# A three-block sequence model on one core: the softmax steps of two attention stages in another order

## The reference, cut to what matters

```python
# sparse attention (nsa_mixer): three softmaxes per head over three kinds of keys
s_c = einsum(q, kc) * scale - slopes * dist_c         # 63 compressed keys, each of 32 tokens
p_c = masked_softmax(s_c, c_end <= t);   o_cmp = p_c @ vc
s   = einsum(q, k_slc) * scale - slopes * dist        # selected keys: the top 16 of 16 blocks, so all up to t
p   = masked_softmax(s, dist >= 0);      o_slc = p @ v_slc
s_w = einsum(q, k_win) * scale - slopes * dist        # window: the last 512 tokens
p_w = masked_softmax(s_w, mask);         o_win = p_w @ v_win
o   = g0 * o_cmp + g1 * o_slc + g2 * o_win

# differential attention (diff_mixer): two softmaxes per head, one per half of the query and key channels
s = einsum('bqhid,bkhid->bhiqk', q, k) * scale - slopes * dist     # i = 0, 1
p = masked_softmax(s, dist >= 0)
a = p[:, :, 0] - lam * p[:, :, 1];       o = a @ v
```

## Time and profile before

| | value |
|---|---|
| three runs, median | 4952.93 us |
| the profiled execution | 4949.35 us, span of the trace 4947.4 us |
| busy in the span: PE, DVE, ACT, POOL | 87%, 38%, 27%, 22% |
| stage nsa in the trace | from 507.8 (first S) to 726.2 (end of the last result) |
| stage diff in the trace | from 753.8 to 943.3 |
| steps in them | 4 x 24 and 4 x 16 |

### The profile page before, as it was taken

One profiled execution on the slowest core, in us unless ns is written; L12 is line 12 of the kernel. 1 busy time (PEld: TensorE's weight loads), 2 busy tenths in 40 slices (PEclk: granted clock), 3 DMA queues, 4 the chain that ended last, 5 costly groups with the idle time before them and its releaser, 6 DMA issues. The chain is left out here.

```text
span 4947.4 us, 55759 instructions
## 1 busy us (share of the span) xinstructions
PE 4315.8 (87%) x21602; PEld 3528.5 (71%) x21602; DVE 1857.7 (38%) x3257; ACT 1335.4 (27%) x2341; POOL 1088.4 (22%) x544
## 2 busy tenths in 40 slices
PE   8997888869983888669999999999899999956897
PEld 6886666757772777456887887888688888845675
DVE  3031565662475665225234234000033333345432
ACT  3120322342213444312000003112143444442121
POOL 2220001241231655211222221221111111122320
PEclk9997999969996999889999999999999999968898
DMA  3233101221323110211111112332243342265422
GB/s 118 100 137 84 35 18 43 76 94 35 137 94 130 37 39 25 82 43 38 57 43 51 44 43 77 113 130 81 87 100 89 107 108 82 82 207 160 143 82 81
DMA packets 277875, 412.06 MB, mean 83 GB/s; under 512 B 52853, under 2 KB 187894, under 8 KB 272122
## 3 DMA queue, kind: packets, MB, share of 16 engines
q1 hardware_dynamic: 206010, 298.36, 19.7%
q10 hardware_dynamic: 69424, 105.53, 5.9%
q0 software_dynamic: 2192, 4.80, 0.4%
HBM read 285.66 MB, written 122.95 MB: 83 GB/s over the span
## 5 line engine op out<-in xcount | busy, mean ns | idle before, releaser
L136 POOL TENSOR_TENSOR weights_wlow<-weights_raw,weights_whigh 128x1024 fp32r<-128x1024 f32 (+1 forms) x236 | 668.0, 2852 | 2582.0 <-ACT weights_whigh L127 2582.0
L260 PE MATMUL acc<-h_high_half,weights_whigh 128*128 128x512 f32 x1440 | 566.3, 393 | 81.0 <-POOL weights_wlow L136 69.2
L127 ACT ACTIVATE weights_whigh<-weights_raw 128x1024 fp32r<-128x1024 f32 (+1 forms) x236 | 267.4, 1163 | 1294.0 <-PE acc L260 653.2
L260 PE MATMUL acc<-h_high_half,weights_wlow 128*128 128x512 f32 x1440 | 564.3, 392 | 0.0
L260 PE MATMUL acc<-h_low_half,weights_whigh 128*128 128x512 f32 x1440 | 564.3, 392 | 0.0
L260 PEld LDWEIGHTS acc<-h_high_half,weights_whigh 128*128 128x128 f32 x1440 | 273.2, 190 | 142.7 <-POOL weights_wlow L136 70.9
L3158 PE MATMUL acc<-h_high_half,weights_whigh 128*128 128x512 f32 x768 | 332.3, 433 | 0.0
L263 PE MATMUL acc<-weights_whigh,h_high_half 128*128 128x512 f32 x768 | 303.4, 395 | 13.9 <-PEq L189 13.9
L260 PEld LDWEIGHTS acc<-h_high_half,weights_wlow 128*128 128x128 f32 x1440 | 273.4, 190 | 56.5
L260 PEld LDWEIGHTS acc<-h_low_half,weights_whigh 128*128 128x128 f32 x1440 | 272.7, 189 | 57.3
L3158 PE MATMUL acc<-h_low_half,weights_whigh 128*128 128x512 f32 x768 | 302.9, 394 | 0.0
(11 more groups left out here) (526 smaller groups left out, 8094.7 us busy)
## 6 DMA issues: line engine op xcount, KB each, us to landing
weights_raw<-w_cols SPq DMA_DIRECT2D x94, 512.0 KB, 4.9
weights_raw<-w_ff SPq DMA_DIRECT2D x64, 512.0 KB, 3.8
weights_raw<-w_rows SPq DMA_DIRECT2D x30, 1024.0 KB, 7.2
att<-gated_result_sb SPq DMA_DIRECT2D x96, 130.0 KB, 2.3
weights_raw<-w_out SPq DMA_DIRECT2D x24, 512.0 KB, 3.8
cols<-cols1p_out ACTq DMA_DIRECT2D x40, 256.0 KB, 2.1
rows<-rows1p_out ACTq DMA_DIRECT2D x32, 256.0 KB, 2.6
x<-x_here SPq DMA_DIRECT2D x2, 4096.0 KB, 14.4
```

Source lines behind the costliest of these rows:

```text
L127: self.core.nc.scalar.activation(high[p][:, half * (KC // 2):(half + 1) * (KC // 2), :], raw[half], ACT.Copy).then_inc(self.core.sem("roun ...
L136: self.core.nc.gpsimd.tensor_tensor(low[p][:, hs, :], raw[half], high[p][:, hs, :].bitcast(F32), ALU.subtract).then_inc(self.core.sem("wei ...
L260: mm = nc.tensor.matmul(core.acc[b][:, :], wt[p][:, k, c * P:(c + 1) * P], h[:, k, half * HALF:(half + 1) * HALF], start=first, stop=final)
```

## The change

Only the two lists of steps are put in another order; every step stays as it was, and so does `attention`. In nsa the list becomes s0, c0, w0, s1, c1, w1, ..., s7, c7, w7: tile by tile, with selected, compressed and window keys in turn. In diff it becomes a0, b0, a1, b1, ..., a7, b7.

```diff
@@ nsa_attention, steps(p)
                                pieces=1, out=lambda it, t=t: [att[t * P:(t + 1) * P, ds(it * HD, HD)]]))
-            for t in range(NT):
+                st.append(dict(queries=q[p][:, t * P:(t + 1) * P], keys=[(kT["cmp"][:, :], 0)],
+                               masks=[(unseen[:, t, :], 0)], width=P, values=[(0, P, val["cmp"][:, :])],
+                               scale=HD ** -0.5, valid=valid[:, 0:1] if t == 0 else None,
+                               pieces=1, out=lambda it, t=t: [att[t * P:(t + 1) * P, ds(it * HD + 8 * HD, HD)]]))
                 t0 = max(0, t - 4)
                 w = (t + 1 - t0) * P
                 st.append(dict(queries=q[p][:, t * P:(t + 1) * P],
...
-            for t in range(NT):
-                st.append(dict(queries=q[p][:, t * P:(t + 1) * P], keys=[(kT["cmp"][:, :], 0)],
-                               masks=[(unseen[:, t, :], 0)], width=P, values=[(0, P, val["cmp"][:, :])],
-                               scale=HD ** -0.5, valid=valid[:, 0:1] if t == 0 else None,
-                               pieces=1, out=lambda it, t=t: [att[t * P:(t + 1) * P, ds(it * HD + 8 * HD, HD)]]))
             return st
@@ diff_attention, steps(p)
-            for i in range(2):
-                for t in range(NT):
+            for t in range(NT):
+                for i in range(2):
                     w = (t + 1) * P
```

## The result

The changed kernel took 4970.45 us (median of 9 runs, 4964.14 to 4974.97), the kernel before in the same rounds 4954.18 (9 runs, 4945.42 to 4957.02): 1.0032 times the time, 95% interval 1.0021 to 1.0042, so 16 us slower, 10 to 21. 4964 was forecast, with 4956 to 4975 as the range, and slower as the likeliest.

What follows compares the result with a forecast made beforehand. TensorE's work plus its waits was taken to bound both stages: nsa +15.2, diff -0.5, half-speed stretches -2, sum +12.7 us on 4949.35, that is 4962.0, or 4965.6 for a median; 4964.0 was given, range 4956 to 4975.

Steps and rivals of the forecast that it cites:

- The rule of covers: Both stages: TensorE waits by how much a step's softmax chain exceeds neighbouring steps' TensorE work; new nsa idle 9.6 us an iteration.
- T(s7): Transposes of nsa's last, widest selected step: chain 2.90 us against cover 1.22, so a wait of 1.68 us.
- T(s0): Transposes of nsa's first selected step, in the new order: a wait of 0.71 us.
- The old idle time: TensorE's idle time in nsa before the change, which the new order removes: 5.8 us an iteration (5.1 to 6.6).
- the 0.7 for store waits: nsa's compressed run before: waits for stored results, taken as 0.7 us an iteration beyond other waits, going away.
- diff: Differential attention stage: idle 2.1 us an iteration before, 2.0 to 2.1 after; net -0.5 us for four (-2 to +1).
- The half-speed stretches: After starts and loop turns at 1.2 GHz, slower matmuls grow into new idle time: 0.5 us each, -2 (0 to -4).
- The gain of the compressed run: Rival: the end of each nsa iteration gets faster and decides, 20 us in all, giving 4933 us; chance 0.04.
- Cancelling: Rival: gains and losses nearly cancel across store waits, half-speed stretches and chains: +5, 4954 to 4958 us; chance 0.17.
- The clock: Rival: waits in every nsa tile drop the clock once an iteration, adding 8 to 12 us: 4972 to 4976; chance 0.09.
- The signs: New trace: nsa exponential waits from 12.7 to some 30 us, no stored-result waits, iteration some 4 us longer, diff's within 0.3.
- signs of being wrong: Last three selected steps' transposes start without waits over 1 us, clock falls mid-iteration, or a stage after 945 us moves.

Runs made afterwards that it cites:

- e7: The kernel before (old order) with four result tiles in place of two: 4945.03 against 4953.08 us, ratio 0.9981.
- e2: The kernel before with the new order in diff alone: 4953.06 against 4951.88 us, ratio 1.0003.
- e9: The changed kernel with four result tiles in place of two: 4965.51 us against 4951.50 for the kernel before, ratio 1.0028.
- e1: The kernel before with the new order in nsa alone: 4967.51 against 4951.88 us, ratio 1.0032.
- e3: The kernel before with nsa's selected and window steps tile by tile, compressed steps as one run at the end: 4954.02 against 4951.88 us, ratio 1.0006.
- e5: The kernel before, with the row maximum of selected steps reading every fourth score: 4951.80 against 4953.08 us, ratio 1.0000.
- e8: The kernel before with nsa tile by tile as selected, window, compressed: 4958.43 against 4953.08 us, ratio 1.0013.
- e6: The changed kernel, with the row maximum of selected steps reading every fourth score: 4956.44 us, ratio 1.0007 to the kernel before.
- e10: Both stages with wide steps beside wide ones, plus four result tiles: 4927.83 us against 4951.50 for the kernel before, ratio 0.9953.
- e4: The kernel before with both stages reordered, wide steps beside wide ones: 4929.58 against 4951.88 us, ratio 0.9953.

## Why the prediction was right, point by point

*The rule of covers* held to within 0.1 us at each step, and to 0.02 from T(s3) to T(s7). Idle time in the fourth iteration, from one start to the next, with the forecast behind it: T(s1) 0.61 (0.67), T(s2) 0.72 (0.80), T(s3) 0.95 (0.93), T(s4) 1.08 (1.06), T(s5) 1.21 (1.19), T(s6) 1.45 (1.44), T(s7) 1.70 (1.68), T(s0) 0.78 (0.71), T(w7) 0.35 (0.32), M(w7) 0.75 (0.66). With 0.19 at T(c0) the sum is 9.8 us, where 9.6 was said.

*The old idle time* was sized too high at 5.8 us. Summed the same way the fourth iteration before has some 5.4, and its length says so too: 57.35 us with 9.8 idle leaves 47.55 of work, and 52.9 less 47.55 is 5.4. The second iteration, 52.6, has 5.1 by the same sum, in which 2 us at half speed stand as well. The term that was off is the 0.7 for store waits that was added to the 5.1. e7 shows that these waits are worth more, 1.5 to 1.7 us an iteration (52.6 and 52.9 against 51.17), but also that nearly all of it had already been counted in the 5.1, which was read from rows that have these waits in them: without them 51.17 less 47.55 leaves 3.6. So an iteration lengthened by 4.7 and 4.4 where +3.8 was forecast and +4.5 was the upper bound. The four iterations of nsa lengthened by 4.2, 4.7, 3.9 and 4.4, in sum 17.2, where +15.2 and a share of the -2 stood. The mechanism was right and the total came out some 4 to 5 us too low (+12.7 against +16 by the medians and +18.1 in the two stages), inside a range that was wide enough for it.

*diff*: -0.5 forecast, within -2 to +1; +0.9 in the trace, and no difference in e2. "The same within 0.3" for an iteration was a little too strict: the second lasts 0.6 longer, 46.0 us, and holds one wait of 1.2 us for a stored result, which the kernel before doesn't have there.

*The half-speed stretches.* The iterations with the start and the first turn in them grew by some 0.4 to 0.8 us less than the plain ones (+4.2 and +3.9 against +4.7 and +4.4), about the 0.5 each that was said. But the two traces don't have equal stretches at half speed: 3.9 us at the start and 10.2 around the turn before, 6.4 and 3.4 in the changed kernel, so this agreement may be luck. A cleaner pair is e7 and e9, with 3.4 us behind the turn in both: the third iteration, with the turn, grew by 5.4 us (55.70 to 61.11) and the plain ones by 6.2. The 0.8 less fits slower matmuls that grow into the idle time. At the start no pair has equal stretches. In diff nothing of the kind is seen.

*The rivals.* The gain of the compressed run is real, 5.1 to 5.4 us an iteration with what hangs on it, but 9.8 us came in its place. Cancelling didn't come. The clock did not fall in mid-iteration in any trace of this order (the changed kernel, e1, e9); what it did elsewhere stands in the last section.

*The signs.* Those of the waits came as written: 30.9 us for exponentials, T(s5) to T(s7) over 1 us each, no wait for a stored result in nsa. Of the signs of being wrong, the last came by the letter, since the stages after 945 us moved by 7.7 in the profiled execution; but the twelve traces of all versions lie between 4001.9 and 4011.8 us there, in no order that follows the steps.

## What to carry to other kernels

In a software pipeline of depth one, what hides a step's latency is the neighbours' work on the busy engine: here T(k-1) + M(k-2) + S(k+1). Write the two sums, chain and cover, for each place of the list before reordering it: a short step beside a long one exposes the long one, so put long steps beside long ones and don't put short ones in a row either: here such a step took 1.03 us with 0.78 us of TensorE's work in it (e7), and some 1.1 with two result tiles. The order alone was worth 38 us between the worst and the best list here (4967.5 against 4929.6), with no instruction added or removed.

## What the runs showed of the hardware beyond that

The granted clock falls to its half, 1.2 GHz, around the end of a run of compressed steps with store waits, and not each time. In e2, whose nsa stage is that of the kernel before, it fell at the end of the first iteration as well:

```profile
545.00:557.70 12.70, 11.12 (x88) 9.82 (x88) 10.37 (x47) 4.89 (x20) 0.00 (x0) 1.00 0.10 23
557.70:564.50 6.80, 5.58 (x20) 4.50 (x20) 2.69 (x11) 1.12 (x5) 1.01 (x2) 0.50 0.21 55
```

and again for 10.2 and 3.4 us at the ends of the second and third, so that the same stage took 221.1 us there and 218.4 in the profile of before. In e3 and e5, with the same run at the end, it fell 2.5 and 2.7 us behind the first S of the second iteration, for 6.8 us. In the three traces of the change's order in nsa (the changed kernel, e1 and e9), with pauses of up to 1.7 us in every tile but no thin run, the clock fell only behind the turn of the loop, for 3.4 us. In e8, which has no run of compressed steps either, it fell once inside a trip of the loop, at 564.0, just behind a pause at T(s0) of the second iteration. VectorE's X(c7), ahead of R(s0), had waited there for a stored result:

```profile
561.56 0.16 DVE L956 RECIPROCAL nsa_total<-nsa_total 128x1 f32<-128x1 f32 x1 [0.86 <-DMA att<-nsa_result]
...
562.98 0.33 PE L841 MATMUL acc<-ident_here,nsa_probs 128*128 128x128 f32 x1 [1.71 <-ACT nsa_probs L895]
```

```profile
553.00:564.00 11.00, 8.99 (x72) 7.88 (x70) 6.33 (x25) 4.15 (x12) 1.01 (x2) 1.00 0.17 41
564.00:567.40 3.40, 3.40 (x14) 3.04 (x13) 2.01 (x10) 1.02 (x4) 0.00 (x0) 0.50 0.04 10
```

So the run of short steps is not needed for a fall. All five traces in which the clock fell elsewhere than behind the turn (before, e2, e3, e5, e8) have store waits of some 0.5 to 2.1 us at the ends of iterations of nsa; the changed kernel, e1, e6, e7, e9 and e10 have none in nsa and no such fall, nor has e4, whose waits at these ends are 0.3 us at most. That the two go together does not make one the cause: in e2 the clock fell at 557.7, just before the wait of 2.1 us began.

The Trainium skill ("TensorE: Matmul & The Clock Gate", section "HAM oscillation — how this bites in real kernels") warns of waits that recur in each tile and drop the clock each time. The three traces of the change's order do not bear this out for pauses of up to 1.7 us; in the other traces the clock fell in some iterations and not in others. What exactly decides whether it falls was not tried.
